# A six-phase encoder kernel: h kept in SBUF across three phases, first loads reordered, scores computed from parts

## The chip, the core and the metric

The kernel runs on one core of a Trainium2 chip. The metric is the device time of one execution in microseconds (us); the median of three runs is shown. All instruction times below come from one profiled execution of the kernel before.

## The reference, cut to what matters

```python
def trunk(x, mem, ...):
    h = rmsnorm(x, norm_g[l])
    proj = jnp.einsum('btd,de->bte', h, w_in[l])
    (g_q, g_k, g_v, g_lr, z_a, d_q, d_k, d_v, z_b, c_q, z_c, gate_in) = jnp.split(proj, offsets, axis=-1)
    o_a = gla_branch(g_q, g_k, g_v, g_lr, ...) * jax.nn.silu(z_a)
    o_b = diff_attention(d_q, d_k, d_v, ...) * jax.nn.silu(z_b)
    o_c = memory_cross_attention(c_q, mem, ...) * jax.nn.silu(z_c)
    branches = jnp.stack([o_a, o_b, o_c], axis=2)
    gates = jax.nn.sigmoid(gate_in.reshape(B, T, N_BRANCH, D))
    merged = jnp.sum(gates * jnp.einsum('btiw,iwd->btid', branches, w_branch[l]), axis=2)
    x = x + jnp.einsum('btd,de->bte', merged, w_out[l])
    return rmsnorm(x, final_norm_g)

def diff_attention(q, k, v, ...):           # 4 heads, two score maps of 64 channels each
    s = jnp.einsum('ibhqd,ibhkd->ibhqk', qblk, kh) + bias
    p = jax.nn.softmax(s, axis=-1)
    a = p[0] - lam * p[1]
    return jnp.einsum('bhqk,bhkv->bhqv', a, vh)
```

Two sequences of 512 and 2048 tokens (2560 in all) and 2 x 256 memory rows; D is 1024, all fp32, one layer. gla_branch is a gated linear attention that scans the tokens forward and backward.

## The kernel before

**Phases.** `build` runs six phases one after the other, with a barrier between them: `phase_project` (0 to 831 us), `phase_gla_forward` (835 to 1988), `phase_gla_backward` (1992 to 2312), `phase_diff` (2316 to 3151), `phase_cross` (3154 to 3276) and `phase_merge` (3279 to 3859). In a phase each engine runs a program written out by hand; semaphores tie them. SP issues nearly all loads and most stores in program order, each `dma_start` held back by the `wait_ge` ahead of it, so whatever stands behind a waiting load waits too. ACT issues the stores of the projection.

**Products.** Large products split each fp32 operand into a high and a low fp32r part and make three matmuls of 512 columns for one (`product3`, L114 to L116): high x high, low x high, high x low. The high part of a weight is a copy, the low one a subtraction on POOL.

**`phase_project`** goes through 5 chunks of 512 tokens. For each chunk ACT squares four x tiles (L243), DVE normalises them (L311), PE transposes them (L368), and ACT and DVE make h_hi (L252) and h_lo (L318). The units of a chunk are one "narrow" unit (the 32 gate-rank columns, in a 128-wide block), 8 "values" units whose weights stay resident, and 16 "stream" units, each with a 512 KB weight piece loaded by `load_piece` (L213) into one of two raw buffers (SLOTS = 2; the wait is on `lo_split`, two pieces back), split by DVE (L329) and POOL (L359). `load_x` (L208) of the next chunk's tiles stands between pieces on SP. A memory part of 8 units follows. hT_hi and hT_lo go to DRAM.

**`Dense`** computes the gate and z projections, 180 units of 24 products (L571), inside both GLA phases, interleaved with the scan. `load_h` loads a chunk of hT with 16 DMAs (L481, L482), `load_w` (L489) one weight block. Both phases take the chunks in order 0 to 4. `begin_transfers` issues the weight block 0, h chunk 0, weight blocks 1 to 3 and h chunk 1, after the phase's own loads.

**`phase_gla_forward`** has 20 tiles of 128 tokens; the o section of a tile (L766, L767) makes, for each of four heads in turn, att x v over 128 rows and Q x state over the head's 64 rows. PE waits for all constants (five loads, `consts_in`) and for DVE's copy of `sums` (L860) before its first matmul, the gate logits (L720).

**`phase_diff`** goes through groups of 4 turns, a turn being 128 queries of one head against T keys: 4 groups of the short sequence (T = 512), then 16 of the long one (T = 2048, 4 key chunks of 512 a turn). For a chunk PE computes the two score maps (L1360) as two fp32 matmuls of 64 rows each, which sit in the two row halves of the array; DVE adds the bias and takes the maximum (L1489), ACT takes the exponentials (L1436), POOL and DVE combine the two maps (L1319, L1323, L1519), PE transposes the result (L1374) and multiplies by v (L1385). The transposes are evacuated by ACT (L1430), every fourth by DVE (L1506). POOL scales q (`scale_q`). Whole heads of q and k are loaded at once; every engine first waits for all constants, `gain` (L1480) the last.

**`phase_cross`** and **`phase_merge`**: cross waits for all its constants before the first score (L1644). Merge adds 12 items (4 blocks of each branch, hi and lo, 24 loads of 256 KB a chunk, L1827 and L1828) weighted by gates; its first product waits for the first items.

## Time and profile before

| | |
|---|---|
| median of 3 runs | 3866.7 us (3863.07 to 3869.71) |
| the profiled execution: time, span | 3861.25 us, 3859.3 us |
| mean granted TensorE clock | 0.967 |
| busy: PE | 3568.4 us (92%), 17304 matmul records |
| busy: PE weight load | 2618.0 us (68%), overlaps PE |
| busy: DVE | 1881.8 us (49%) |
| busy: ACT | 1290.0 us (33%) |
| busy: POOL | 1246.5 us (32%) |
| moved by DMA | 542.81 MB, 141 GB/s |

The span runs from the first to the last instruction. PE busy includes stretches at the lower clock level, in which a matmul lasts about twice as long. An fp32 matmul shows as two records. In the rows, L12 is line 12 of the kernel before; PE is the matmul queue, SPq the issue of DMAs by SP, and the brackets give the idle time before an instruction and what ended it.

### The profile page before, as it was taken

How to read it: one execution, taken by the hardware profiler on the slowest of the kernel's cores; microseconds unless marked ns; L12 is line 12 of the kernel's file. 1: busy time of each engine (PE TensorE's matmuls, PEld its weight loads, DVE VectorE, ACT ScalarE, POOL GpSimd, SP SyncE). 2: the span in 40 equal slices, each digit the busy share in tenths (PEclk: the TensorE clock that was granted, in tenths of full speed). 3: DMA queues.
4: the chain of work that ended last, by engine and by line, in shares of the span. 5: the costliest groups of instructions: out<-in, count | busy, mean ns of one | idle time of the engine just before them, and what ended most of it. 6: DMA issues, size and time to landing. Idle time of an engine off the chain costs nothing. (4 is left out here: it accounts for less than half of the span.)

```text
span 3859.3 us, 46682 instructions
## 1 busy us (share of the span) xinstructions
PE 3568.4 (92%) x17304; PEld 2618.0 (68%) x17304; DVE 1881.8 (49%) x4161; ACT 1290.0 (33%) x2132; POOL 1246.5 (32%) x518
## 2 busy tenths in 40 slices
PE   6999999969999999999978986899999968899998
PEld 5778778758888888888866762344444435688887
DVE  4211211214333433433327786888888846555555
ACT  2111111113333333333322224455555535433332
POOL 2322321423332333233223324666666633200000
PEclk9999999989999999999989997999999989899999
DMA  5434434364343433433348873010110024866662
GB/s 178 147 140 148 153 142 145 136 215 146 124 161 113 161 124 119 150 127 115 110 151 279 284 214 132 28 39 28 39 36 17 17 96 164 309 205 216 214 206 98
DMA packets 304237, 542.81 MB, mean 141 GB/s; under 512 B 31595, under 2 KB 110571, under 8 KB 302604
## 3 DMA queue, kind: packets, MB, share of 16 engines
q1 hardware_dynamic: 258300, 469.29, 36.4%
q10 hardware_dynamic: 45712, 70.55, 5.1%
q8 instruction: 138, 2.26, 0.3%
q14 instruction: 87, 0.71, 0.1%
HBM read 380.07 MB, written 159.67 MB: 140 GB/s over the span
## 5 line engine op out<-in xcount | busy, mean ns | idle before, releaser
L555 POOL TENSOR_TENSOR glaf_w_lo<-glaf_raw,glaf_w_hi 128x1024 fp32r<-128x1024 f32 x140 | 351.8, 2513 | 807.1 <-ACT glaf_w_hi L525 807.1
L571 PE MATMUL glaf_dense_acc<-glaf_h_hi,glaf_w_hi 128*128 128x512 f32 x1120 | 451.8, 403 | 1.8 <-DMA glaf_h_lo<-scratch_hT_lo 1.8
L571 PE MATMUL glaf_dense_acc<-glaf_h_hi,glaf_w_lo 128*128 128x512 f32 x1120 | 439.8, 393 | 0.0
L571 PE MATMUL glaf_dense_acc<-glaf_h_lo,glaf_w_hi 128*128 128x512 f32 x1120 | 439.2, 392 | 0.0
L1489 DVE CUSTOM_DVE_ANT_0 diff_p<-diff_s_ps,diff_table 128x512 f32<-128x512 f32 x544 | 352.6, 687 | 108.2 <-PE diff_s_ps L1360 104.9
L359 POOL TENSOR_TENSOR proj_w_lo<-proj_raw,proj_w_hi 128x1024 fp32r<-128x1024 f32 x84 | 203.9, 2432 | 535.6 <-DVE proj_w_hi L329 535.6
L1360 PE MATMUL diff_s_ps<-diff_k,diff_q 64*128 64x512 f32 x1088 | 317.7, 664 | 32.6 <-DMA diff_gain<-in_diff_gain 23.0
L1319 POOL TENSOR_SCALAR diff_p<-diff_p,diff_ratio 128x1024 f32<-128x1024 f32 (+1 forms) x80 | 268.1, 3351 | 228.9 <-DVE diff_ratio L1516 228.8
L1385 PE MATMUL diff_oT_ps<-diff_aT,diff_v 128*128 128x512 f32 x544 | 290.3, 634 | 10.1 <-ACT diff_aT L1430 7.6
L114 PE MATMUL proj_acc<-proj_h_hi,proj_w_hi 128*128 128x512 f32 x672 | 269.0, 400 | 17.9 <-POOL proj_w_lo L359 17.9
L1436 ACT ACTIVATE diff_p<-diff_p,diff_neg_max 128x2048 f32<-128x2048 f32 (+1 forms) x160 | 278.4, 1741 | 15.0 <-DVE diff_neg_max L1499 14.9
L268 ACT ACTIVATE proj_out<-proj_acc 128x512 f32<-128x512 f32 x133 | 79.6, 598 | 601.0 <-PE proj_acc L116 601.0
L901 DVE COPY_PREDICATED glaf_att<-glaf_picked,glaf_att_ps 128x256 f32<-128x256 int32 x280 | 147.3, 526 | 270.2 <-PE glaf_att_ps L702 263.3
L1374 PEld LDWEIGHTS diff_t_ps<-diff_ident,diff_a 128*128 128x128 f32 x1088 | 131.6, 143 | 203.5 <-issue 147.0
L115 PE MATMUL proj_acc<-proj_h_lo,proj_w_hi 128*128 128x512 f32 x672 | 266.6, 397 | 0.0
L116 PE MATMUL proj_acc<-proj_h_hi,proj_w_lo 128*128 128x512 f32 x672 | 266.0, 396 | 0.0
L571 PEld LDWEIGHTS glaf_dense_acc<-glaf_h_hi,glaf_w_hi 128*128 128x128 f32 x1120 | 211.0, 188 | 45.9 <-issue 5.7
L571 PEld LDWEIGHTS glaf_dense_acc<-glaf_h_hi,glaf_w_lo 128*128 128x128 f32 x1120 | 210.8, 188 | 40.3
L571 PEld LDWEIGHTS glaf_dense_acc<-glaf_h_lo,glaf_w_hi 128*128 128x128 f32 x1120 | 211.2, 189 | 35.8
L868 DVE TENSOR_TENSOR glaf_K<-glaf_X,glaf_qk 128x1024 f32<-128x1024 f32 x80 | 118.1, 1477 | 219.1 <-ACT glaf_X L810 219.1
L1430 ACT ACTIVATE diff_aT<-diff_t_ps 128x512 f32<-128x512 f32 x208 | 122.8, 592 | 271.9 <-PE diff_t_ps L1374 271.1
L114 PE MATMUL merge_acc<-merge_br_hi,merge_w_hi 128*128 128x512 f32 x480 | 191.3, 398 | 22.6 <-DMA merge_br_lo<-scratch_item_lo 11.3
(199 smaller groups left out, 7055.2 us busy)
## 6 DMA issues: line engine op xcount, KB each, us to landing
glaf_raw<-in_w_zg SPq DMA_DIRECT2D x140, 512.0 KB, 3.6
proj_raw<-in_w_stream SPq DMA_DIRECT2D x80, 512.0 KB, 3.5
scratch_zg<-glaf_dense_out SPq DMA_DIRECT2D x140, 256.0 KB, 2.2
merge_raw<-in_w_br SPq DMA_DIRECT2D x120, 256.0 KB, 3.0
merge_gate<-scratch_zg SPq DMA_DIRECT2D x120, 256.0 KB, 3.6
scratch_featT<-proj_out ACTq DMA_DIRECT2D x80, 256.0 KB, 2.0
glab_raw<-in_w_zg SPq DMA_DIRECT2D x40, 512.0 KB, 4.9
merge_br_hi<-scratch_item_hi SPq DMA_DIRECT2D x60, 256.0 KB, 6.0
```

The costliest lines, as they stand in the source:

```text
L114: pe.matmul(out, a_hi, b_hi, start=first, stop=False)
L115: pe.matmul(out, a_hi, b_lo, start=False, stop=False)
L116: return pe.matmul(out, a_lo, b_hi, start=False, stop=last)
L359: pool.tensor_tensor(lo, raw[:, n % SLOTS], hi, ALU.subtract).then_inc(lo_split, 1)
L555: pool.tensor_tensor(self.w_lo[:, s], self.raw[:, u % self.RAW], self.w_hi[:, s], ALU.subtract).then_inc(self.lo_split, 1)
L571: done = pe.matmul(self.acc[:, u % self.BANKS], a, x, start=i == 0, stop=i == self.PER - 1)
L901: dve.copy_predicated(queries(att[:, :, :, :].rearrange("p z a t -> p (z a) t"), n, d), picked[:, d, n].rearrange("p (n m) -> p n m", m=ha ...
L1319: pool.tensor_scalar(p[:, o.slot, 1, half], p[:, o.slot, 1, half], ratio[:, o.slot:o.slot + 1], None, ALU.mult).then_inc(far_scaled, 1)
L1360: done = pe.matmul(s_ps[:, chunk % 2, i], q[r, n.head % 2, n.tile * P:(n.tile + 1) * P], k[r, n.head % 2, c * KC:(c + 1) * KC], start=True ...
L1385: pe.matmul(oT_ps[:, :], v[:, o.head % 2, kt], aT[:, unit % 2], start=kt == 0, stop=kt == o.nk - 1).then_inc(values_done, 1)
L1436: act.activation(p[:, o.slot, i, 0:o.T], p[:, o.slot, i, 0:o.T], ACT.Exp, bias=neg_max[:, o.slot, i:i + 1], scale=SLOPES[o.h], accum_out=s ...
L1489: dve.tensor_tensor_reduce(out=p[:, n.slot, i, c * KC:(c + 1) * KC], in0=s_ps[:, (n.c0 + c) % 2, i], in1=table[:, start:start + KC], scale ...
```

## The change

One diff touches all six phases.

- **h handed over.** `h` (hi and lo, two chunk buffers) is allocated once and passed to the projection and both GLA phases. `Dense` gets `held`, the number of chunks that it finds in place: forward takes the chunks as 4, 0, 1, 2, 3 and finds chunk 4 there; backward takes 3, 2, 4, 0, 1 and finds two. `load_w(0)` moves to the start of each pass. In forward, 20 products of the first unit are issued ahead of the wait for `sums`, and the waits for constants are split by constant.
- **Projection.** Resident weights come first and the narrow one last, in the order of pieces and of units; four raw buffers in place of two; ACT makes the high parts of the residents; in chunk 0 a values unit waits for its own x tile alone. The narrow unit becomes 16 matmuls (below), with `glr` stored as 64 rows and `w2` doubled to match. For the 8 blocks of d_q and d_k ACT writes the high part (q with its scale folded in), DVE a low part (`low_part`, 40 instructions of 128x512), and ACT stores that too (40 DMAs of 256 KB to `featT_lo`).
- **GLA forward.** The o section goes by pairs of heads: att, att, Q, Q. The gate logits contract 65 rows in place of 33.
- **Diff.** Scores from parts: two full-height fp32r matmuls and two half-height ones per chunk. q is loaded per group and k per chunk, 5 DMAs each (L1325 to L1346 of the changed kernel); `scale_q` goes; ACT does all transposes' evacuations; the bias table comes in three loads, with waits for each constant where it is used.
- **Cross and merge.** First q tile and memory first; merge's 24 first item loads are issued during cross (`Items`); merge starts with weights, gates and w_o.

```diff
 # phase_project
+            units += [("values", c, v, t) for v in range(2) for t in range(TT)]
             units += [("narrow", c, 0, 0)]
-            units += [("values", c, v, t) for v in range(2) for t in range(TT)]
...
-        STREAM, MEMC = N_FEAT, TOK // CH
+        STREAM, MEMC, RAW, NR = N_FEAT, TOK // CH, 4, 2 * RANK
...
             def load_piece(n):
-                if n >= SLOTS:
-                    sp.wait_ge(lo_split, n - SLOTS + 1)
-                sp.dma_start(raw[:, n % SLOTS], source(n)).then_inc(raw_in[n % SLOTS], 16)
+                if n >= RAW:
+                    sp.wait_ge(lo_split, n - RAW + 1)
+                sp.dma_start(raw_of(n), source(n)).then_inc(raw_in[n % RAW], 16)
...
+            def low_part(u):
+                i, n = units[u][2], part_units.index(u)
+                scale = HD ** -0.5 / SLOPES[i - DQ_BLOCK] if i < DK_BLOCK else 1.0
+                dve.wait_ge(evacuated, u + 1)
+                if n >= 2:
+                    dve.wait_ge(low_stored[n % 2], 16 * (n // 2))
+                dve.scalar_tensor_tensor(out_lo[:, n % 2], acc[:, u % BANKS], scale, out[:, u % OUTS], ALU.mult, ALU.subtract).then_inc(low_out, 1)
...
+                if kind == "narrow":
+                    both, high = acc[0:2 * NR, u % BANKS], acc[0:NR, u % BANKS]
+                    pe.matmul(both, wn[:, 0], h_hi[:, b, 0], start=True, stop=False)
+                    pe.matmul(high, wn[:, 0, 0:NR], h_lo[:, b, 0], start=False, stop=False)
+                    for k in range(1, KT):
+                        pe.matmul(high, wn[:, k, 0:NR], h_lo[:, b, k], start=False, stop=False)
+                        done = pe.matmul(both, wn[:, k], h_hi[:, b, k], start=False, stop=k == KT - 1)
 # phase_gla_forward
-                for h in range(H):
-                    r = head_rows(h)
-                    cols = slice(h // 2 * GV, (h // 2 + 1) * GV)
-                    pe.matmul(o_ps[:, h % 2, cols], att[:, h % 2, h // 2], v[:, b, h], start=True, stop=False)
-                    done = pe.matmul(o_ps[:, h % 2, cols], Q[r, 0, h // 2, INTER - 1], state[r, h // 2], start=False, stop=True)
+                for a in range(PAIRS):
+                    cols = slice(a * GV, (a + 1) * GV)
+                    for h in (2 * a, 2 * a + 1):
+                        pe.matmul(o_ps[:, h % 2, cols], att[:, h % 2, a], v[:, b, h], start=True, stop=False)
+                    for h in (2 * a, 2 * a + 1):
+                        r = head_rows(h)
+                        done = pe.matmul(o_ps[:, h % 2, cols], Q[r, 0, a, INTER - 1], state[r, a], start=False, stop=True)
 # phase_diff, scores
+                for i in range(2):
+                    pe.matmul(s_ps[:, chunk % 2, i], q_both[:, b, i, cols], k_both[:, key % KS, i], start=True, stop=False)
                 for i in range(2):
                     r = slice(HD * i, HD * (i + 1))
-                    done = pe.matmul(s_ps[:, chunk % 2, i], q[r, n.head % 2, n.tile * P:(n.tile + 1) * P],
-                                     k[r, n.head % 2, c * KC:(c + 1) * KC], start=True, stop=True)
+                    done = pe.matmul(s_ps[:, chunk % 2, i], q_high[r, b, cols], k_low[r, key % KS], start=False, stop=True)
 # phase_diff, ACT
-                if ku > 2:
-                    evacuate(o, 2)
+                for c in range(2, ku):
+                    evacuate(o, c)
 # phase_cross, SP
+            load_z(1)
+            items.load(sp, 0, 2 * H)
...
+                if c == 2:
+                    sp.wait_ge(stored[0], 32 * H)
+                    items.load(sp, 2 * H, 3 * H)
```

How the order of instructions moves at three places follows. First, PE in `phase_diff`, in a turn of the long sequence. Before:

```order
L1374 MATMUL diff_t_ps<-diff_ident,diff_a 128x128 x4
L1360 MATMUL diff_s_ps<-diff_k,diff_q 128x512 x2
L1385 MATMUL diff_oT_ps<-diff_aT,diff_v 128x512 x2
L1374 MATMUL diff_t_ps<-diff_ident,diff_a 128x128 x4
L1360 MATMUL diff_s_ps<-diff_k,diff_q 128x512 x2
```

And now (`q_both` holds q's high and low part in the two row halves, `k_both` k's high part twice):

```order
L1464 MATMUL diff_t_ps<-all_ident,diff_a 128x128 x4
L1448 MATMUL diff_s_ps<-diff_k_both,diff_q_both 128x512 x2
L1451 MATMUL diff_s_ps<-diff_k_low,diff_q_high 128x512 x2
L1475 MATMUL diff_oT_ps<-diff_aT,diff_v 128x512 x2
L1464 MATMUL diff_t_ps<-all_ident,diff_a 128x128 x4
```

The transposes and the products with v stand where they stood; each chunk's two score instructions have become four.

Second, PE in `phase_gla_forward`, the o section of one tile. Before:

```order
L766 MATMUL glaf_otd_ps<-glaf_v,glaf_att 128x128
L767 MATMUL glaf_otd_ps<-glaf_state,glaf_Q 128x128
L766 MATMUL glaf_otd_ps<-glaf_v,glaf_att 128x128
L767 MATMUL glaf_otd_ps<-glaf_state,glaf_Q 128x128
L766 MATMUL glaf_otd_ps<-glaf_v,glaf_att 128x128
L767 MATMUL glaf_otd_ps<-glaf_state,glaf_Q 128x128
L766 MATMUL glaf_otd_ps<-glaf_v,glaf_att 128x128
L767 MATMUL glaf_otd_ps<-glaf_state,glaf_Q 128x128
```

And now:

```order
L838 MATMUL glaf_otd_ps<-glaf_v,glaf_att 128x128 x2
L841 MATMUL glaf_otd_ps<-glaf_state,glaf_Q 128x128 x2
L838 MATMUL glaf_otd_ps<-glaf_v,glaf_att 128x128 x2
L841 MATMUL glaf_otd_ps<-glaf_state,glaf_Q 128x128 x2
L845 MATMUL glaf_otd_ps<-glaf_v,glaf_k_tok 64x128 x4
```

The same eight instructions alternate between the two shapes four times in place of eight.

Third, SP at the start of `phase_gla_backward`. Before:

```order
L977 DMA glab_o<-scratch_gla_o 128x512
L489 DMA glab_raw<-in_w_zg 128x1024
L481 DMA glab_h_hi<-scratch_hT_hi 128x512
L482 DMA glab_h_lo<-scratch_hT_lo 128x512
L481 DMA glab_h_hi<-scratch_hT_hi 128x512
```

And now:

```order
L562 DMA glab_raw<-in_w_zg 128x1024
L1049 DMA glab_qb<-scratch_qb 128x256
L1050 DMA glab_kb<-scratch_kb 128x256
L1051 DMA glab_dec<-scratch_decb 128x2
L1052 DMA glab_v<-scratch_gla_v 128x512
L1053 DMA glab_o<-scratch_gla_o 128x512
L1069 DMA glab_gain<-in_gla_gain 128x128
```

The first weight block (L489, now L562) is SP's first load of the phase; the 32 loads of h chunks at its start are gone.

## Rows read from the trace of the kernel before

**Rows 1.** Windows: length, busy us (instructions) of PE, PEld, DVE, ACT, POOL, clock, DMA share, GB/s.
```profile
860.00:1990.00 1130.00, 1123.89 (x6828) 916.41 (x6826) 419.45 (x558) 377.59 (x654) 348.05 (x139) 1.00 0.40 130
...
3275.00:3300.00 25.00, 11.62 (x28) 6.79 (x29) 4.66 (x8) 4.95 (x7) 0.00 (x0) 0.64 0.93 337
```

**Rows 2.** Timeline, PE, start of projection: start us, length us, line, operation, count, [idle before].
```profile
16.58 1.94 PE L368 MATMUL proj_tp<-proj_ident,proj_xn 128*128 128x128 f32 x8 [16.58 <-DVE proj_xn L311]
...
42.04 0.77 PE L114 MATMUL proj_acc<-proj_h_hi,proj_wn_hi 128*128 128x512 f32 x1 [2.85 <-issue]
```

**Rows 3.** Timeline, SP, the x load of a chunk boundary in the projection.
```profile
109.06 11.21 SPq L213 DMA_DIRECT2D proj_raw<-in_w_stream  x3
120.31 0.43 SPq L208 DMA_DIRECT2D proj_x<-in_x_all  x1
```

**Rows 4.** Timeline, PE, the same boundary, between chunks 0 and 1.
```profile
129.60 1.09 PE L368 MATMUL proj_tp<-proj_ident,proj_xn 128*128 128x128 f32 x8 [2.08 <-DVE proj_xn L311]
133.10 0.77 PE L114 MATMUL proj_acc<-proj_h_hi,proj_w_hi 128*128 128x512 f32 x1 [2.41 <-POOL proj_w_lo L359]
```

**Rows 5.** Windows, the same boundary.
```profile
129.00:137.00 8.00, 4.99 (x17) 4.00 (x18) 3.04 (x5) 1.08 (x2) 5.05 (x2) 0.64 0.47 157
```

**Rows 6.** Groups of 50 to 830 us, one line: | busy us, mean ns | idle before.
```profile
L114 PE MATMUL proj_acc<-proj_h_hi,proj_w_hi 128*128 128x512 f32 x672 | 269.0, 400 | 17.9 <-POOL proj_w_lo L359 17.9
```

**Rows 7.** Timeline, PE, the o section of one tile in phase_gla_forward.
```profile
1528.79 0.39 PE L571 MATMUL glaf_dense_acc<-glaf_h_hi,glaf_w_lo 128*128 128x512 f32 x1
1529.02 0.38 PE L766 MATMUL glaf_otd_ps<-glaf_v,glaf_att 128*128 128x128 f32 x2
1529.33 0.49 PE L767 MATMUL glaf_otd_ps<-glaf_state,glaf_Q 64*128 64x128 f32 x2
...
1532.25 0.66 PE L771 MATMUL glaf_otd_ps<-glaf_v,glaf_k_tok 128*64 128x128 f32 x8
```

**Rows 8.** Timeline, PE, where each later stage starts, and one gap inside phase_gla_backward.
```profile
845.53 1.19 PE L720 MATMUL glaf_z_ps<-glaf_decay_w,glaf_glr 33*128 33x512 f32 x1 [14.49 <-DVE glaf_sums L860]
...
2014.42 0.76 PE L571 MATMUL glab_dense_acc<-glab_h_hi,glab_w_hi 128*128 128x512 f32 x1 [14.66 <-DMA glab_h_lo<-scratch_hT_lo]
...
2048.94 0.47 PE L571 MATMUL glab_dense_acc<-glab_h_hi,glab_w_hi 128*128 128x512 f32 x1 [2.51 <-DVE glab_dense_out L540]
...
2328.35 6.34 PE L1360 MATMUL diff_s_ps<-diff_k,diff_q 64*128 64x512 f32 x16 [22.99 <-DMA diff_gain<-in_diff_gain]
...
3165.85 1.62 PE L1644 MATMUL cross_s_ps<-cross_kT,cross_q 128*128 128x256 f32 x3 [18.97 <-DMA cross_q<-scratch_featT]
...
3284.19 0.76 PE L114 MATMUL merge_acc<-merge_br_hi,merge_w_hi 128*128 128x512 f32 x1 [11.31 <-DMA merge_br_lo<-scratch_item_lo]
```

**Rows 9.** Timeline, PE, part of a long-head turn in phase_diff.
```profile
2704.37 0.60 PE L1374 MATMUL diff_t_ps<-diff_ident,diff_a 128*128 128x128 f32 x4
2704.90 1.13 PE L1360 MATMUL diff_s_ps<-diff_k,diff_q 64*128 64x512 f32 x4
2705.96 0.66 PE L1374 MATMUL diff_t_ps<-diff_ident,diff_a 128*128 128x128 f32 x4
...
2707.61 1.13 PE L1385 MATMUL diff_oT_ps<-diff_aT,diff_v 128*128 128x512 f32 x2
2708.57 0.60 PE L1374 MATMUL diff_t_ps<-diff_ident,diff_a 128*128 128x128 f32 x4
```

**Rows 10.** Timeline, PE, the closing gaps of two successive groups in phase_diff.
```profile
2494.80 0.66 PE L1374 MATMUL diff_t_ps<-diff_ident,diff_a 128*128 128x128 f32 x4 [1.67 <-DVE diff_a L1519]
...
2539.08 0.66 PE L1374 MATMUL diff_t_ps<-diff_ident,diff_a 128*128 128x128 f32 x4 [1.67 <-DVE diff_a L1519]
```

**Rows 11.** Windows, long heads.
```profile
2500.00:2600.00 100.00, 96.66 (x387) 42.65 (x385) 83.64 (x242) 54.44 (x71) 60.57 (x23) 1.00 0.10 38
```

**Rows 12.** Costliest groups of one such group of turns: two lines of ACT.
```profile
L1436 ACT ACTIVATE diff_p<-diff_p,diff_neg_max 128x2048 f32<-128x2048 f32 x8 | 16.0, 1997 | 0.0
...
L1430 ACT ACTIVATE diff_aT<-diff_t_ps 128x512 f32<-128x512 f32 x12 | 7.1, 592 | 14.3 <-PE diff_t_ps L1374 14.3
```

More of the change, by code:

```diff
@@ L135, in phase_project @@
         first_unit = [min(u for u, x in enumerate(units) if x[1] == c) for c in range(NC + 1)] + [len(units)]
-        pieces = [("narrow", 0, 0, 0)] + [("values", 0, v, col) for v in range(2) for col in range(COLS)]
+        pieces = [("values", 0, v, col) for v in range(2) for col in range(COLS)] + [("narrow", 0, 0, 0)]
         RESIDENT = len(pieces)
@@ L181, in phase_project, with in_parts @@
         evacuated = m.sem("evacuated")
+        low_out = m.sem("low_out")
+        low_stored = m.sems("low_stored", 2)
         stored = m.sems("stored", OUTS)
         block = m.block()
+        def in_parts(u):
+            kind, c, i, _ = units[u]
+            return kind == "stream" and c < MEMC and DQ_BLOCK <= i < CQ_BLOCK
+        part_units = [u for u in range(len(units)) if in_parts(u)]
         def source(n):
@@ L201, in split_into, with raw_of @@
             return w_hi[:, s], w_lo[:, s]
+        def raw_of(n):
+            return raw[:, n % RAW, :, 0:NR] if pieces[n][0] == "narrow" else raw[:, n % RAW]
         @block.sync
@@ L277, in evacuate, with high_resident @@
                     dst = memkT[i] if c == MEMC else featT[i, :, cols]
-                act.dma_start(dst, out[:, u % OUTS]).then_inc(stored[u % OUTS], 16)
+                act.dma_start(dst, out[0:2 * NR if kind == "narrow" else P, u % OUTS]).then_inc(stored[u % OUTS], 16)
+            def high_resident(n):
+                act.wait_ge(raw_in[n % RAW], 16 * (n // RAW + 1))
+                act.activation(split_into(n)[0], raw_of(n), ACT.Copy).then_inc(hi_resident, 1)
             square(0)
+            high_resident(0)
+            high_resident(1)
             square(1)
-            for n in range(TT):
-                high(n)
-                if n + 2 < TT:
-                    square(n + 2)
+            high(0)
+            high_resident(2)
+            high_resident(3)
+            square(2)
+            high(1)
+            high_resident(4)
+            high_resident(5)
+            square(3)
             for u, (kind, c, i, t) in enumerate(units):
@@ L347, in _ @@
                     split(n)
+                if u and in_parts(u - 1):
+                    low_part(u - 1)
                 j, r = divmod(at, 6)
@@ L566, in products @@
                     pe.wait_ge(self.evacuated, u - self.BANKS + 1)
-                if u in self.first_of:
-                    pe.wait_ge(self.h_in[b], 32 * KT * (index // self.buffers + 1))
+                if u in self.first_of and index >= self.held:
+                    loads = sum(i % self.buffers == b for i in range(self.held, index + 1))
+                    pe.wait_ge(self.h_in[b], 32 * KT * loads)
             a = (self.w_hi, self.w_hi, self.w_lo)[part][:, s, k]
@@ L1210, in phase_diff @@
         NORM_STEPS = 2 + RSQRT_STEPS
-        by_dve = [c % 4 == 3 for n in units for _ in range(G) for c in range(n)]
-        dve_before = [sum(by_dve[:i]) for i in range(len(by_dve) + 1)]
-        def wait_aT(engine, unit):
-            if by_dve[unit]:
-                engine.wait_ge(aT_dve, dve_before[unit] + 1)
-            else:
-                engine.wait_ge(aT_act, unit - dve_before[unit] + 1)
         class Turn:
@@ L1557, in _, with phase_cross @@
                     maximum(n)
-                if late and not (n.live and n.units > 3):
-                    evacuate(o, 3)
                 if e:
                     combine(e)
-def phase_cross(nc, featT, kT_dram, v_dram, ident_dram, zg, item_hi, item_lo):
+def phase_cross(nc, ident, items, featT, kT_dram, v_dram, zg, item_hi, item_lo):
     with ExitStack() as ctx:
```

400 lines of the change are left out of this document (237 added, 163 removed).

## The prediction

> **What bounds the kernel now.** I first read the windows by stage, to see which engine is full and at which clock. In the forward GLA pass PE is busy 1123.89 of 1130 us at full clock [rows 1]; time can go there only if PE gets less to do. Around the first 25 us of merge it is busy 11.62 us at a mean clock of 0.64, with the DMA share at 0.93 [rows 1]: there loads decide. Then I read the timeline of PE at the start of each stage for the idle time and its releaser [rows 2, 8], and at a chunk boundary of the projection [rows 3 to 5]. Last come the long heads of diff, where PE is busy 96.66 of 100 us, DVE 83.64, POOL 60.57 and ACT 54.44 [rows 11]: PE bounds, and DVE is second with little room. So the kernel is PE-bound with a dozen stalls between, and PE pays for a stall twice, since it also comes back at half clock: after the stall at 133.10 the pitch of products is 0.57 and then 0.43 us, and the window shows 0.64 [rows 4, 5].
>
> **The sum, by places.** All against the span of 3859.3 us.
>
> *Start of the projection.* The first transposes start at 16.58 and the first product at 42.04, after all four x tiles [rows 2]. Now the first values unit needs one tile and four weight pieces. Transposes 1.94 us plus the two h parts put the tile at about 21; the high parts of the weights move to ACT and no longer queue behind DVE's normalising. I take 23, so -19. The ends are -21 (nothing but the tile) and -8 (POOL's low parts come at today's rhythm).
>
> *Chunk boundaries.* SP's load of the next x tile is issued only at 120.31, after 11.21 us of waiting for a raw buffer [rows 3]; PE then lacks 2.08 and 2.41 us [rows 4], and of 8 us a share of 0.36 goes to the clock, 2.9 us [rows 5]. With four buffers SP is two units further ahead, more than the stall. Five boundaries x 7.4 = -37. DVE's new low parts fall in stream units and have room: POOL and DVE wait there. The wait new on PE (a bank whose low part must be taken) is three units old by then: nothing.
>
> *Memory part.* Of the idle time ahead of these products, 17.9 us [rows 6], five boundaries explain 12; the rest, 5.9, is weight pieces late in the memory part: -6 with deeper buffers.
>
> *Narrow unit.* Eight matmuls fewer in each of five chunks, at a pitch of 0.23 from 1528.79 to 1529.02 [rows 7], is -9. But they now alternate between 64 and 32 columns, 15 changes a unit. The nearest row with changes of shape is the o section, where a pair of records takes 0.40 ((1532.25 - 1529.02) / 8) against 0.21 for two records of 0.107, which is the pitch of transposes (0.43 for four [rows 9], with the change 0.53): 0.1 to 0.2 a change, of which I take the o section's 0.2. 75 x 0.2 = +15, so +6 in sum; it is the same kind of change though not the same shapes. Ends -9 and +6.
>
> The Trainium skill, "TensorEngine Tiling (Array Packing)", Key Properties, says that a change of tiling mode (not of tile) drains TensorE; by that rule the narrow unit and the split scores each pay, and the o section gains. It speaks against two parts of this change; the sum by it is the sum here, as the rows already carry the price of 0.2. No row before shows a change of columns alone.
>
> *Projection to forward GLA.* PE is idle 14.49 us to 845.53, released by DVE's copy of `sums`, which waited for the last constant [rows 8]. The logits need only `decay_w` and the gates now, and 20 products follow at once; their weights come fourth in SP's queue. How early the weights arrive is not shown; I take two thirds of the idle time: -10. Ends -3 and -15.
>
> *o section, 20 tiles.* Eight pairs of 0.40 = 3.2 us [rows 7]. Now four changes x 0.2, four att products x 0.21, and the Q products, two row halves at once, 2 x 0.21: 2.1. PE is full here, so 20 x 1.1 = -22 (ends -16, if the two halves don't run at once, and -24). The logits' 65 rows no longer run beside their neighbours: 20 x 0.1 = +2.
>
> *Start of backward GLA.* The idle 14.66 us ended by h_lo [rows 8] go: both h chunks are there, and the weights are first in the queue: -14. Inside the phase about half of the eight gaps (2 to 4 us each, as the one at 2048.94) follow the first two h loads, gone: -8.
>
> *Diff, start.* 22.99 us, released by `gain`, the last of the constants [rows 8]. q, k and the near part of the table are still loaded, now as 10 DMAs for one turn in place of whole heads: -5, and -2 in the short heads.
>
> *Diff, long heads.* From 2704.37 four transposes take 0.53 with the change to row halves, of which 0.43 are theirs; the scores take 1.06 to 2705.96; the next transposes have 0.06 of exposed weight load either way: 1.16 a chunk. A change to a full-height matmul costs no drain (0.96 for two fp32 matmuls of 512 columns, 2707.61 to 2708.57) [rows 9]. Now: two full matmuls x 0.23, change 0.2, one pair at 0.23, change back 0.1: 0.99. Saved 0.17 x 256 chunks = -44. Groups repeat every 44.28 us, with a closing gap of 1.67, fourteen times [rows 10]; the period should fall to 41.5. Ends: the pair one after the other, +0.23 a chunk, in all +14; and no load exposed, -60. DVE at 37.0 of 44.28 us loses four copies and stays near 83% of the shorter period. ACT takes those over: 16.0 us of exponentials and 16 x 0.59 of copies [rows 12], 26.5 of 41.5 in all. POOL loses `scale_q`, which was off the path.
>
> *Cross and merge.* Cross waits 18.97 us for its q [rows 8], issued fifth; now it is first: -5 (the barrier and the transfer stay). Merge waits 11.31 us for item low parts [rows 8] and then runs at 0.64 [rows 1]. 24 loads are now done during cross; what remains is the first weights: -17, ends -8 and -22. The new wait in cross (`stored[0]`, then four items) is on SP, with the z load and stores behind it, and they have a whole chunk's time.
>
> Sum: -19 - 37 - 6 + 6 - 10 - 22 + 2 - 14 - 8 - 7 - 44 - 5 - 17 = **-181**. Span 3678, time 3680 (the profiled execution took 1.95 more than its span, 3861.25). The median of the runs is 5.4 above the profiled execution, so I forecast **3685 us**.
>
> **Rivals.**
> 1. *The long heads give nothing.* Either the fp32r row halves run one after the other, or DVE's bias chain takes over as the bound when PE gets faster. For: DVE is at 84%, and no row shows fp32r in row halves. Against: fp32 halves run at once (four records in 0.96). Time 3685 + 44 = 3729, up to 3743. Chance 0.15.
> 2. *The boundary stalls stay.* Something besides x is late (DVE's `norm` behind more `low_part`), so the 37 us stay: 3722. Against: the window shows DVE idle over half of the time there. Chance 0.08.
> 3. *First loads only swap places.* At each of the five stage starts the barrier and one DMA chain remain, and half of the 51 us stays: 3711. Chance 0.12.
> 4. *Narrow changes are free*: 3670. Chance 0.08.
> 5. *Slower: ACT holds up diff.* The fourth transposes' copy now stands behind both exponentials (2.0 us each [rows 12]) in ACT's queue; PE's product with v waits for it, and PE's own queue with the next scores behind that. If one exponential comes in the way in each of 64 turns, 128 us are lost: 3813, still faster. From 2.9 us a turn the change is slower, and with both, 4.0 x 64 = 256, it is 3941. For: ACT's third copy today already stands there, and PE's waits on copies are short. ACT has 35% room in the mean, so I give it 0.03.
> 6. *The hold of h or items is not effective* (the loads wait on the same semaphore as before, or the buffers cost a wait elsewhere): 3720, chance 0.02.
>
> **The numbers.** The forecast has 0.52. Its own range, from the ends of the terms, is 3655 to 3710. To leave out no more than 2 in 10 I take 3645 to 3735, which holds rivals 1 to 4 with nearly all of their chance. A measurement of this kernel tells 0.2%, some 8 us, from no change; only rival 5 comes near or above it. Faster by over 0.2%: 0.96; within 0.2%: 0.015; slower: 0.025.
>
> **What would show it.** In the profile after: a first product near 23 us; no gap over 1 us at the four inner chunk boundaries and clock 1.00 in them; the narrow unit at about 6.7 us or 3.7 (rival 4); the o section at 2.1 us; backward GLA's first dense product right after its first deltas; groups of long turns every 41.5 us (44.3 is rival 1), with PE busy still above 95%; merge's first product some 5 us after cross. A wait of PE's products with v on ACT's copy, over 1 us a turn, would be rival 5. The forecast is wrong if the span is over 3730, or if it is right in sum with two of these places wrong.

## The result and the profile after

The changed kernel takes **3696.06 us** (median of 4 runs, 3694.17 to 3701.03) against 3865.26 us before: a ratio of 0.9563, 95% interval 0.9546 to 0.9579. I had forecast 3685 us with a range of 3645 to 3735. The profiled execution has a span of 3695.6 us, 163.7 less than before, where the sum had said 181. One execution of the changed kernel in run 9 took 5738.88 us at a mean granted clock of 0.556, and every comparison leaves it out. Measured between PE's first and last instructions of each stage (the last row goes on to the end of the span), the time went here:

| stretch of PE's timeline | before, us | after, us | change | forecast |
|---|---|---|---|---|
| start to the first product | 42.0 | 23.1 | -19.0 | -19 |
| projection, first to last product | 789.0 | 743.7 | -45.3 | -37 |
| on to the first dense product of forward GLA | 25.3 | 14.5 | -10.8 | -10 |
| forward GLA from there | 1131.5 | 1120.0 | -11.5 | -20 |
| on to PE's last instruction of backward GLA | 317.5 | 292.2 | -25.4 | -22 |
| wait ahead of diff | 23.0 | 20.0 | -3.0 | -5 |
| diff | 818.5 | 789.6 | -28.9 | -46 |
| wait ahead of cross | 19.0 | 12.3 | -6.7 | -5 |
| cross and merge | 693.5 | 680.2 | -13.3 | -17 |

The page of the changed kernel, busy time by engine: PE's share rises, but its busy time falls by only 83 us of the 164; the rest was idle time.

```profile
PE 3485.7 (94%) x17264; PEld 2628.7 (71%) x17264; DVE 1858.3 (50%) x4128; ACT 1332.0 (36%) x2205; POOL 1221.9 (33%) x510
```

PE's timeline at the starts of the stages, after (to be held against [rows 2, 8]):

```profile
23.09 0.78 PE L118 MATMUL proj_acc<-proj_wv_hi,h_hi 128*128 128x512 f32 x1
...
48.52 1.97 PE L428 MATMUL proj_tp<-all_ident,proj_xn 128*128 128x128 f32 x8 [6.49 <-DVE proj_xn L365]
...
773.84 2.04 PE L789 MATMUL glaf_z_ps<-glaf_decay_w,glaf_glr 65*128 65x512 f32 x2 [7.07 <-DMA glaf_decay_w<-in_w]
781.26 0.79 PE L643 MATMUL glaf_dense_acc<-h_hi,glaf_w_hi 128*128 128x512 f32 x1 [5.37 <-POOL glaf_w_lo L626]
798.36 0.69 PE L807 MATMUL glaf_z_ps<-glaf_sums,glaf_L_hi 128*128 128x384 f32 x1 [9.65 <-ACT glaf_X L884]
...
1912.70 1.22 PE L1112 MATMUL glab_o_ps<-glab_state,glab_qb 64*128 64x128 f32 x8 [11.46 <-DVE glab_state L1149]
...
1914.91 0.80 PE L643 MATMUL glab_dense_acc<-h_hi,glab_w_hi 128*128 128x512 f32 x1
...
2213.40 1.19 PE L1448 MATMUL diff_s_ps<-diff_k_both,diff_q_both 128*128 128x512 f32 x2 [19.98 <-DMA diff_k_low<-scratch_featT_lo]
...
3015.37 2.90 PE L1747 MATMUL cross_s_ps<-cross_kT,cross_q 128*128 128x256 f32 x6 [12.32 <-DMA cross_kT<-scratch_memkT]
...
3135.98 0.79 PE L118 MATMUL merge_acc<-items_br_hi,merge_w_hi 128*128 128x512 f32 x1 [10.47 <-DVE merge_w_lo L2120]
```

The 14.66 us ahead of the first dense product of backward GLA are gone: it follows the phase's first scan matmuls with no idle time. The wait ahead of those scan matmuls stays, 11.46 us at 1912.70 (9.67 before), and the forecast had no term for it. At the other starts a wait remains, with another releaser: merge no longer waits for items but 10.47 us for the split of its first weights. Two rows are new stalls: 6.49 us at 48.52, where the first x tile of chunk 1 is late, and 9.65 us at 798.36. SP issues the load of that x tile at 31.14, behind a weight piece, and ACT can square the tile only from 38.60.

The windows of the changed kernel for the whole steady projection, and for four successive groups of the long heads and a later one (length, busy us with instruction counts of PE, PEld, DVE, ACT, POOL, then clock, DMA share, GB/s):

```profile
60.00:760.00 700.00, 700.00 (x3164) 575.55 (x3163) 171.93 (x413) 118.59 (x203) 213.96 (x88) 1.00 0.48 169
```

```profile
2452.54:2494.15 41.61, 39.94 (x171) 21.26 (x171) 34.19 (x99) 26.28 (x35) 27.52 (x11) 1.00 0.12 35
2494.15:2540.38 46.23, 44.56 (x171) 23.97 (x171) 33.55 (x99) 26.39 (x35) 27.54 (x11) 0.89 0.20 58
2540.38:2581.96 41.58, 39.91 (x171) 21.26 (x171) 34.21 (x99) 26.28 (x35) 27.54 (x11) 1.00 0.13 40
2581.96:2625.82 43.86, 40.48 (x170) 21.30 (x171) 34.18 (x99) 26.29 (x35) 27.49 (x11) 1.00 0.36 110
...
2708.95:2755.23 46.28, 44.62 (x171) 23.93 (x171) 33.55 (x99) 26.39 (x35) 27.51 (x11) 0.89 0.11 34
```

In the projection PE is busy 700 of 700 us at full clock: every boundary stall is gone [rows 4, 5]. In diff a plain group takes 41.58 us, as forecast (41.5). But three of this profile take 46.2 at a clock of 0.89, and the one in which the head changes takes 43.9. These are what the forecast of diff lacked. A closer look at the group that begins at 2494, in 2 us windows:

```profile
2492.00:2494.00 2.00, 0.48 (x2) 0.00 (x0) 1.87 (x5) 1.23 (x2) 1.13 (x1) 1.00 1.01 288
2494.00:2496.00 2.00, 1.85 (x10) 1.17 (x11) 0.13 (x2) 1.16 (x2) 2.00 (x1) 0.87 1.00 308
2496.00:2498.00 2.00, 2.00 (x8) 1.24 (x6) 1.27 (x4) 2.00 (x4) 1.85 (x2) 0.50 0.99 288
```

The idle time of 1.67 us ahead of the group's first transposes is the one of [rows 10]; before the change the full clock held across it 14 times. Now the clock falls to 1.2 GHz after 4 of the 14: three times for about 10 us, which costs 4.6, and once, at 2927, for about 7, which costs 3.3.

How the scores now lie in a turn of the long heads (PE's timeline, to be held against [rows 9]), the o section (against [rows 7]) and a part of the narrow unit:

```profile
2703.88 0.60 PE L1464 MATMUL diff_t_ps<-all_ident,diff_a 128*128 128x128 f32 x4
2704.24 0.70 PE L1448 MATMUL diff_s_ps<-diff_k_both,diff_q_both 128*128 128x512 f32 x2
2704.87 0.50 PE L1451 MATMUL diff_s_ps<-diff_k_low,diff_q_high 64*128 64x512 f32 x2
2705.30 1.98 PE L1475 MATMUL diff_oT_ps<-diff_aT,diff_v 128*128 128x512 f32 x4
```

```profile
1288.03 0.60 PE L838 MATMUL glaf_otd_ps<-glaf_v,glaf_att 128*128 128x128 f32 x4
1288.57 0.49 PE L841 MATMUL glaf_otd_ps<-glaf_state,glaf_Q 64*128 64x128 f32 x4
1288.99 0.71 PE L838 MATMUL glaf_otd_ps<-glaf_v,glaf_att 128*128 128x128 f32 x4
1289.63 0.49 PE L841 MATMUL glaf_otd_ps<-glaf_state,glaf_Q 64*128 64x128 f32 x4
1290.05 0.66 PE L845 MATMUL glaf_otd_ps<-glaf_v,glaf_k_tok 128*64 128x128 f32 x8
```

```profile
78.12 0.39 PE L450 MATMUL proj_acc<-h_hi,proj_wn 128*64 128x512 f32 x1
78.35 0.40 PE L451 MATMUL proj_acc<-h_lo,proj_wn 128*32 128x512 f32 x1
...
81.58 0.39 PE L454 MATMUL proj_acc<-h_hi,proj_wn 128*64 128x512 f32 x1
81.81 0.38 PE L428 MATMUL proj_tp<-all_ident,proj_xn 128*128 128x128 f32 x2
```

From the start of the transposes to the end of the scores a chunk takes 0.36 + 1.06 us where it took 0.53 + 1.06: the saving of 0.17 stands between the transposes and the scores. Within the 1.06 the two full-height matmuls take 0.63 and the pair in the row halves 0.43. The trace puts the two starts of the pair 0.004 us apart (2704.870 and 2704.874), so the halves run at once; how the 0.43 divides into a change of shape and the products no run shows. The o section takes 2.02 us in place of 3.23, and 20 of them give -24. The narrow unit takes 3.69 us, 16 times 0.23: its 15 changes of width cost nothing.

### The profile page after: what moved, and what is told of

The parts are those of the page before. It is cut to its first block and busy times, and to the rows that moved or that the text cites. A ratio compares the mean times of both kernels' runs of the same rounds, so it can differ in the third digit from the quotient of the medians.

```text
span 3695.6 us, 46898 instructions
## 1 busy us (share of the span) xinstructions
PE 3485.7 (94%) x17264; PEld 2628.7 (71%) x17264; DVE 1858.3 (50%) x4128; ACT 1332.0 (36%) x2205; POOL 1221.9 (33%) x510
## 5 line engine op out<-in xcount | busy, mean ns | idle before, releaser
L643 PE MATMUL glaf_dense_acc<-h_hi,glaf_w_hi 128*128 128x512 f32 x1120 | 452.7, 404 | 5.4 <-POOL glaf_w_lo L626 5.4
L643 PE MATMUL glaf_dense_acc<-h_hi,glaf_w_lo 128*128 128x512 f32 x1120 | 440.2, 393 | 0.0
L643 PE MATMUL glaf_dense_acc<-h_lo,glaf_w_hi 128*128 128x512 f32 x1120 | 439.7, 393 | 0.0
L118 PE MATMUL proj_acc<-h_hi,proj_w_hi 128*128 128x512 f32 x672 | 262.8, 391 | 0.0
L120 PE MATMUL proj_acc<-h_hi,proj_w_lo 128*128 128x512 f32 x672 | 261.6, 389 | 0.0
L119 PE MATMUL proj_acc<-h_lo,proj_w_hi 128*128 128x512 f32 x672 | 261.5, 389 | 0.0
L643 PEld LDWEIGHTS glaf_dense_acc<-h_hi,glaf_w_hi 128*128 128x128 f32 x1120 | 211.4, 189 | 51.2 <-POOL glaf_w_lo L626 6.9
L643 PEld LDWEIGHTS glaf_dense_acc<-h_hi,glaf_w_lo 128*128 128x128 f32 x1120 | 211.4, 189 | 41.2
L643 PEld LDWEIGHTS glaf_dense_acc<-h_lo,glaf_w_hi 128*128 128x128 f32 x1120 | 211.7, 189 | 36.0
L1448 PE MATMUL diff_s_ps<-diff_k_both,diff_q_both 128*128 128x512 f32 x544 | 204.9, 459 | 31.0 <-DMA diff_k_low<-scratch_featT_lo 24.0
```

Of the source, the lines that this page charges most:

```text
L118: pe.matmul(out, a_hi, b_hi, start=first, stop=False)
L119: pe.matmul(out, a_hi, b_lo, start=False, stop=False)
L120: return pe.matmul(out, a_lo, b_hi, start=False, stop=last)
L643: done = pe.matmul(self.acc[:, u % self.BANKS], a, x, start=i == 0, stop=i == self.PER - 1)
L1448: pe.matmul(s_ps[:, chunk % 2, i], q_both[:, b, i, cols], k_both[:, key % KS, i], start=True, stop=False)
```

## The experiments

The ratio of each run is taken to the kernel before on the same chip. "Span" is that of the profiled execution, the changed kernel's is 3695.6, and where nothing else is said a difference in span is against that one profile. Diff alone, with the changed kernel's scores and waits, takes 778.2 to 791.1 us in nine profiles, so I also give the stage that an edit touches.

**1. The projection's raw buffers alone, in the kernel before** (RAW is 4).

```diff
-                if n >= SLOTS:
-                    sp.wait_ge(lo_split, n - SLOTS + 1)
-                sp.dma_start(raw[:, n % SLOTS], source(n)).then_inc(raw_in[n % SLOTS], 16)
+                if n >= RAW:
+                    sp.wait_ge(lo_split, n - RAW + 1)
+                sp.dma_start(raw[:, n % RAW], source(n)).then_inc(raw_in[n % RAW], 16)
```

> The kernel before, with four raw buffers for weight pieces in the projection in place of two, nothing else. Theory (the x loads were late because SP stood in a wait for a raw buffer): the idle times of 2.1 and 2.4 us and the half-clock stretch at the five chunk boundaries go, and the stalls of the memory part too; first to last product of the projection falls from 789 us to about 746, the span from 3859 to 3816. Rival (what was late was DVE or POOL work of the boundary, or the gain came from the other edits of the projection): the gaps stay, span 3859 within 4 us.

Measured: 3810.42 us, ratio 0.9864 (0.9849 to 0.9878), span 3815.7; first to last product 744.1 us. SP's timeline and the window of the first boundary in this kernel:

```profile
109.12 0.43 SPq L208 DMA_DIRECT2D proj_x<-in_x_all  x1
```

```profile
124.00:140.00 16.00, 16.00 (x77) 13.32 (x76) 3.37 (x5) 2.89 (x5) 6.50 (x4) 1.00 0.37 131
```

The x load is issued at 109.12 where it was at 120.31 [rows 3], and the boundary has no idle time. The theory stands: from first to last product the deeper buffering takes off 44.9 us (the span 43.6), 27% of the whole. By the medians, 3810.42 against 3864.53, it is 54 us; the profiled execution was the slowest of the four of this kernel (the other three took 3810), and where the other 10 us lie is not shown. The run also says that the rest of the projection's edits give nothing net between first and last product (744.1 against 743.7): the narrow unit's -9 is used up by the stall of 6.49 at 48.5, the lower clock behind it, and the transposes of two x tiles, which now fall behind the first product.

**2. The o section in its old order**, in the changed kernel (the loop of the kernel before put back, as in the diff of the change).

> The changed kernel with the o section of the forward GLA pass in its old order (att, Q for one head after the other). Theory (a change between full height and row halves costs 0.2 us, and two Q products in different halves run at once): the section goes back from 2.02 to 3.23 us, 20 times, +24 us in a phase in which PE is full: 3720. Rival (PE waits for the scan there, so the time saved became idle time elsewhere): under +8 us, 3696 to 3703.

Measured: 3721.77 us, ratio 0.9631 (0.9615 to 0.9647), span 3721.1: +25.5 (+25.7 by the medians), of which 22 lie in forward GLA. The theory stands.

**3. h not held.**

```diff
-        self.held = held
+        self.held = 0
```

> The changed kernel, in which both GLA passes load all their h chunks again, into the same two buffers and in the changed order of chunks. Theory (holding h is worth the start of the backward pass and part of its inner gaps): forward start +5 (16 more transfers ahead of the rest), backward start +10 to +14, inner gaps +5: 3716 to 3728. Rival (the early first weight block was what mattered, h is loaded in the same time): under +8, up to 3703.

Measured: 3727.42 us, ratio 0.9644 (0.9629 to 0.9658), span 3727.1: +31.5. PE's timeline of this kernel at both starts:

```profile
794.76 0.77 PE L643 MATMUL glaf_dense_acc<-h_hi,glaf_w_hi 128*128 128x512 f32 x1 [18.72 <-DMA h_lo<-scratch_hT_lo]
...
1941.76 0.76 PE L643 MATMUL glab_dense_acc<-h_hi,glab_w_hi 128*128 128x512 f32 x1 [12.39 <-DMA h_lo<-scratch_hT_lo]
```

Forward now waits 18.72 us for h_lo (its first dense product stands 13.5 us later than at 781.26), and the stall at 798 shrinks to 7.5. Backward gets back the 12.39 us ahead of its first product and its last product comes 20 us later after forward's last one than in the changed kernel. The theory stands, at its upper end, with most of the 31 in backward; the forward start cost more than it said, 13.5 us in place of 5.

**4. Merge's first items loaded by merge.** The two `items.load` of cross are left out, and merge issues the 24 loads between its first weights and gates, as the kernel before did.

> The changed kernel with merge's first 24 item loads at the start of merge, in the order that the kernel before had, and none during cross. Theory (the early items are worth merge's first stalls): cross runs 3 us faster (107 in place of 110), merge's first product waits on items again and its later stalls and half-clock stretches come back, from first product to end 575 in place of 560: +12 net, 3708. Rival (the load of the first weights bounds merge's start either way): within 4 us of 3696.

Measured: 3713.73 us, ratio 0.9609 (0.9591 to 0.9626), which is +18 by the medians. The four executions lie in two pairs, 3706.71 and 3708.5, 3718.95 and 3719.81, and the profiled one is the slowest: span 3717.7, +22, of which 20 lie in cross and merge together. PE's timeline after its first product:

```profile
3149.80 0.47 PE L118 MATMUL merge_acc<-items_br_hi,merge_w_hi 128*128 128x512 f32 x1 [2.41 <-DVE merge_w_lo L2123]
...
3171.71 0.79 PE L118 MATMUL merge_acc<-items_br_hi,merge_w_hi 128*128 128x512 f32 x1 [7.48 <-DVE merge_w_lo L2123]
```

The windows of merge's first 50 us, with early items and in this run:

```profile
3135.98:3185.98 50.00, 48.47 (x201) 39.05 (x202) 43.22 (x44) 29.13 (x47) 20.27 (x8) 0.95 0.85 292
```

```profile
3142.08:3192.08 50.00, 38.28 (x126) 27.40 (x127) 22.84 (x29) 20.44 (x33) 12.30 (x5) 0.78 0.93 336
```

Right in direction, somewhat small in size (+12 expected), and right on merge itself: 565.8 us from first to last product, 549.7 with early items, 565.2 in the kernel before. It was wrong on cross, which took 113 us against 110. The first wait hardly differs (11.19 us here, 10.47 with early items, 11.31 in [rows 8]). The gain of the early items lies behind it, where PE now waits 2.41 and 7.48 us for the split of later weights and the clock is 0.78 in place of 0.95. I read from this that the early items free DMA time for those weights.

Cross is no measure of the item loads: in the profiles of all kernels it takes 106.9 to 107.3 us where the clock is at the lower level for some 7 us of it, 109.5 to 111.0 at 10 to 14 us, and 113.1 at 20. The code of the kernel before gives both 107.0 (its own profile) and 110.2 (run 1).

**5. Weight blocks ahead of the h chunk in forward GLA.**

```diff
         self.load_w(sp, 1)
-        for index in range(self.held, self.buffers):
-            self.load_h(sp, index)
         self.load_w(sp, 2)
         self.load_w(sp, 3)
+        for index in range(self.held, self.buffers):
+            self.load_h(sp, index)
```

> The changed kernel with SP issuing weight blocks 2 and 3 of the forward GLA pass ahead of the 16 loads of the h chunk that is needed much later. Theory (ACT stands in its queue in the wait for weight block 2, issued at 786.5 behind those loads and landed at 796.9, with the scan's work behind it, and PE waits for that): the new gap of 9.7 us at 798 goes with its half-clock stretch of some 2 us: span -10 to -12, about 3685. Rival (the DMA engines are full there, share 0.94, and other loads are late in its place): under 4 us, above 3691.

Measured: 3685.61 us, ratio 0.9533 (0.9515 to 0.9551), span 3684.4: -11.2. Forward GLA from its first dense product takes 1110.4 us in place of 1120.0. The rows that had led to the theory, SP's and ACT's timelines of the changed kernel, and then the window of the stall in this run:

```profile
786.50 2.15 SPq L562 DMA_DIRECT2D glaf_raw<-in_w_zg  x2
```

```profile
796.88 1.06 ACT L596 ACTIVATE glaf_w_hi<-glaf_raw 128x1024 fp32r<-128x1024 f32 x1 [11.06 <-DMA glaf_raw<-in_w_zg]
797.84 0.85 ACT L884 ACTIVATE glaf_X<-glaf_z_ps 128x384 f32<-128x384 f32 x2
```

```profile
781.00:799.00 18.00, 17.57 (x73) 14.25 (x73) 9.88 (x11) 8.14 (x14) 7.89 (x3) 0.90 0.73 258
```

PE is busy 17.57 of these 18 us; in the changed kernel it was 8.09. A smaller wait of 2.37 us, for DVE, appears at 816. So the stall was an in-order queue at work twice: the weight load stood behind 16 loads on SP, and the scan's exponentials stood behind the wait for that weight on ACT.

**6. Scores ahead of the transposes where a group opens.**

```diff
+                ahead = bool(o) and o.quarter == 0 and nu > 0
+                if ahead:
+                    scores(n, 0)
                 for c in range(2):
                     if c < ku:
                         transposes(o, c)
-                    if c < nu:
+                    if c < nu and not (ahead and c == 0):
                         scores(n, c)
```

> The changed kernel, in which PE in the turn that opens a group's transposes issues the next turn's first score chunk (1.05 us) ahead of them. Theory (the 1.67 us of idle time at each closing are a wait for DVE's last combination, and the half-clock stretches of 4.6 us after some of them follow from the idle time): the gap falls to about 0.6, 16 times, -17, and the three to five half-clock stretches go, -14 to -23: 3660 to 3668. Rival 1 (DVE, 83% busy, is the chain that sets the group's period): the gap reappears elsewhere, period 41.6, 3696. Rival 2 (the half-clock stretches have nothing to do with this gap): 3679 or so, with the stretches still there.

Measured: 3666.18 us, ratio 0.9478 (0.9457 to 0.95), span 3663.5: -32. PE's timeline at a closing, and the window of all long heads:

```profile
2491.11 1.09 PE L1464 MATMUL diff_t_ps<-all_ident,diff_a 128*128 128x128 f32 x8 [0.77 <-DVE diff_a L1608]
```

```profile
2325.00:2946.00 621.00, 603.28 (x2560) 323.72 (x2559) 525.09 (x1471) 400.63 (x529) 415.74 (x152) 1.00 0.19 57
```

The idle time falls to 0.77, the group from 41.58 to 40.58 us, which is 16 us in all, and the clock is 1.00 over 621 us, where the changed kernel shows 0.97 (559 us, its long heads). The theory stands and both rivals fall: the gap was part of the period, and the half-clock stretches went with it. That this is no chance of one profile is seen over all of them. In nine profiles with the gap of 1.67 us the clock fell after 21 of 126 closings. In the two with 0.77 (this run and run 12) it fell after none of 27. Diff takes 754.6 us here, and 761.7 in run 12.

**7. Without the pair of row halves.** The products of q's high with k's low part are left out, and the full-height matmuls close the accumulation.

> The changed kernel without the two half-height score matmuls of each chunk: the product of q's high part with k's low part is left out of the scores. Theory (PE bounds the long heads, with DVE close behind): the pair costs 0.42 us, so PE would have 41.6 - 16 x 0.42 = 34.9 us of work a group, less than DVE's 34.2 with its waits; the period becomes 36 to 37, -75 us in all, 3620, and DVE's busy share goes to over 0.92. Rival (DVE or ACT already set the period): it stays at 41 or so.

Measured: 3633.57 us in one run, span 3631.5: -64. A plain group takes 38.2 to 39.2 us. The window of 100 us of long heads:

```profile
2500.00:2600.00 100.00, 82.86 (x357) 50.01 (x356) 89.16 (x254) 68.37 (x92) 73.70 (x27) 1.00 0.26 79
```

Of the 6.7 us a group taken off PE about 3 came back as time: neither 36.5, as the theory put it, nor 41. (The theory also called PE's 34.9 us of work less than DVE's 34.2; they are nearly equal.) PE is now idle 17%; in this window it waits 7.9 us for DVE's bias step and 5.9 for DVE's last combination, and DVE is busy 0.89. I read from this that DVE's chain is a bound about 3 us below the present 41.6, without a run of its own to show it. Rival 1 of the prediction had a real wall in it, only further off.

**8. The narrow unit grouped by width** (7 matmuls of 64 columns, 8 of 32, 1 of 64).

> The changed kernel, whose narrow unit issues the 64-column matmuls together and the 32-column ones together (2 changes of width in place of 15). If a change of width cost something beyond what the records show, the unit would fall below its 3.70 us (16 x 0.23); if, as its length suggests, it is free, 3.70 stays.

Measured: 3688.8 us in one run, span 3686.9; first to last product of the projection 744.5 us, against 743.7. The unit is not shorter, 3.70 us: changes of width are free in this kernel. The 8.7 us less in the span come from diff (778.8 us, 10.8 less), where one half-clock stretch follows a closing in place of four.

**9. The changed kernel once more**, as the reference of the next three.

> The changed kernel as it is, on the same chip as the three below, as their reference: 3695 within 6 us. If the half-clock stretches of the long heads are chance events, their places differ from the first profile; if they come with the program, they stand in the same groups.

Measured: 3696.17 us (median of three), ratio 0.9553 (0.9537 to 0.9569), span of the profiled execution 3685.2, with diff at 778.7 us. One long group takes 46.2 us, at another place than those of the first profile, and the plain ones take 41.6 again:

```profile
2664.80:2711.00 46.20, 44.57 (x170) 23.93 (x170) 33.53 (x99) 26.38 (x35) 27.42 (x11) 0.89 0.20 58
```

So the stretches come by chance and not at fixed places: the nine profiles with this gap have one to four each, at changing groups. It is not chance alone, since the two profiles with the old scores (the kernel before and run 1) have none after 28 closings with the same 1.67 us; why they have none is not shown. One profile alone can put diff some 11 us too high or too low.

**10. h chunks handed out in portions.** After each dense unit SP issues 4 of a chunk's 16 loads, and forward starts with weight blocks 1 to 3, as in run 5.

```diff
         self.load_w(sp, 1)
-        for index in range(self.held, self.buffers):
-            self.load_h(sp, index)
         self.load_w(sp, 2)
         self.load_w(sp, 3)
+        self.pending += [(index, k) for index in range(self.held, self.buffers) for k in range(0, KT, 2)]
...
                 if index < len(self.chunks):
-                    self.load_h(sp, index)
+                    self.pending += [(index, k) for k in range(0, KT, 2)]
+            if self.pending:
+                index, k = self.pending.pop(0)
+                self.load_h(sp, index, (k, k + 1))
```

> The changed kernel with each h chunk's 16 loads handed out 4 at a time, one portion after each dense unit, instead of in one run, and weight blocks 2 and 3 first at the start of forward. Theory (a run of 16 loads holds SP and the DMA engines, and weight blocks and tiles behind it come late): the forward gap of 9.7 goes as in the run with weights first (-11), and most of the 13 us of gaps inside the backward pass go too: 3672 to 3678. Rival (backward is full of transfers whatever their order, DMA share 0.8): only the forward part, about 3684.

Measured: 3660.47 us, ratio 0.9467 (0.9451 to 0.9483), span 3659.1: -36 against run 9 by the medians. Forward takes 1112.1 us in place of 1127.4 (first to last matmul) and backward 266.5 in place of 280.7, 30 us together; backward's gaps over 1 us fall from 13.4 us in five to 3.8 in two. The other 6 us are less than diff varies by from profile to profile. Run 5's order alone left forward at 1117.8 and backward at 283.9, so that 23 of the 30 us belong to the portions. The theory stands and gave somewhat too little: every run of 16 loads had cost something, not only the first.

**11. Three loads a piece in diff in place of five.**

```diff
-                for i in range(2):
-                    for half in range(2):
-                        sp.dma_start(k_both[HD * half:HD * (half + 1), s, i].bitcast(FP32), featT[DK_BLOCK + h, HD * i:HD * (i + 1), cols]).then_inc(k_in[s], 16)
+                for half in range(2):
+                    sp.dma_start(k_both[HD * half:HD * (half + 1), s].bitcast(FP32), featT[DK_BLOCK + h, :, cols].rearrange("(i p) t -> p i t", i=2)).then_inc(k_in[s], 16)
...
```

> The changed kernel with q's and k's parts in diff loaded by 3 DMAs a piece in place of 5. Theory (at the three changes of long heads PE waits for k because SP needs 3 us for the five issues of a chunk, more than PE's 2.4 us): the groups at a change of head fall from about 43.5 to 42 us or less, -4 to -6 in all, and the first score of diff comes 2 us earlier: 3688. Rival (the transfers, not their issue, are late): within 2 us of no change.

Measured: 3697.54 us, ratio 0.956 (0.9545 to 0.9576): no difference from run 9. The groups at a change of head take 42.7, 44.1 (48.7 with a half-clock stretch in it) and 42.2 us, where run 9 has 43.1, 43.7 and 42.8, and diff's first score comes after 19.8 us of waiting, not 18. A miss, and the rival stands: the transfers are late, not their issue. At the second change of head SP needs 1.9 us for a chunk in place of 3.0, but the last k load, issued at 2614.60, lands only at 2624.01, 9.4 us later, while PE waits for it. In the first profile of the changed kernel the waited-for loads took 4.2 and 4.5 us to land. The DMA share in 2615 to 2625 is over 1.0 here and 0.85 there. Whether more than the single turn of notice would help was not tried.

**12. Runs 6, 10 and 11 together.**

> Scores ahead of the transposes at a group's opening, h loads spread and weights first, and 3 loads a piece, together. If the gains add up (-32, -20, -7): 3637, and PE over 96% busy. If one of them had only moved a wait that another one meets again: 3645 to 3655.

Measured: **3636.82 us** (3635.49 to 3641.47), ratio 0.9408 (0.9394 to 0.9422). PE is busy 3463.6 of 3635.9 us, 95% and not the 96% expected. The gains nearly add up: -30 (run 6) and -36 (run 10) against -59, by medians. This version beats both kernels.

## Why the forecast was right, and which steps were off

The time, 11 us above the forecast, lies in the range, and the likeliest case was the right one. That the sum came within 17 us of the span is partly luck: the projection gave 8 us more than the sum said, where the narrow unit had been put 15 us too dear, and this hides part of the 8 and 17 us that forward GLA and diff did not give. Of the places named as signs of being wrong, one did not come about: merge's first product stands 10.5 us after cross and not 5. Step by step:

- **Start of the projection (-19):** right; the first product stands at 23.09. Not foreseen was the next wait, 6.49 us at 48.5, for a tile whose load still stands behind a weight piece on SP.
- **Boundaries and memory part (-43):** right in mechanism and size, 44.9 by the stage in run 1.
- **Narrow unit (+6):** wrong. The step that failed is taking the o section's 0.2 us a change for changes of column width. The unit takes 3.69 us: -9, as rival 4 had it. Here the rule of the Trainium skill ("TensorEngine Tiling (Array Packing)", Key Properties) that a change of tiling mode drains TensorE and the trace part: between 64 and 32 columns at full height nothing shows, between full height and row halves it is 0.1 to 0.2 us.
- **Forward GLA (-22 +2):** wrong in size, -11.5 for -20. The o section itself measured -24, and run 2 gives it back. The sum missed a stall of 9.65 us that the change itself makes. I had counted what the early weight block brings and not which later weight block the h loads now push back, and who waits behind it on ACT.
- **Start and inside of backward GLA (-22):** right, -25.4; run 3 gives 20 of it to holding h. The sum left out the 10 us of waiting ahead of the phase's scan, which stayed (9.67 before, 11.46 after).
- **Diff, the scores (-44):** right in its sum, 0.17 us a chunk and 41.58 us a group against a forecast of 41.5, but not in all its parts. The two full-height matmuls take 0.63 us and not 0.46, the transposes ahead of them 0.36 and not 0.43, and no change back shows; the differences cancel, which is luck. The halves run at once, so rival 1 did not come about, and PE's waits on ACT's copies total 4.6 us on the page, so rival 5 did not either. What failed is what I took as fixed: that the closing gap costs 1.67 us and nothing else. Diff gave 28.9 us for 46. Four half-clock stretches took back 17 us in the first profile and groups in which loads come late about 6 (1.1 to 2.3 us each), while the short heads gave some 5 more than forecast. In run 9, with one such stretch, diff gives 39.8. One reading was off as well: the 0.96 us of [rows 9] are one fp32 matmul in two records, not two matmuls. No term changes by it.
- **Cross and merge (-22 with the wait ahead of cross):** -19.9 in sum, and not where I put it. The 11 us of waiting ahead of merge's first product stayed, with the weights' split as releaser; the gain is in the stalls and the clock behind it, 15.5 us within merge (run 4). Cross itself took 3 us more in this profile. Run 4 shows that this is the clock, 12.6 us at the lower level in place of 6.7, and not the item loads.

## What to carry to other kernels

When a load is moved forward in a queue, list what is behind it now and which engine stands in an in-order wait for each of those; the stall of 9.65 us was of this kind by run 5, and handing out such loads in portions took 30 us off the two GLA phases in run 10. A short idle time that repeats is worth filling even where it looks cheap, since the clock may fall after it. And buffers that let the loading queue run further ahead of a wait can be worth more than all the arithmetic saved: two more raw buffers gave 45 of 164 us.

## What the runs showed of the hardware that I had not expected

- fp32r matmuls of 64 rows in the two row halves run at once: the two of a pair start 0.004 us apart, and from a pair of 512 columns to the next instruction it is 0.43 us.
- A change between 64 and 32 columns costs nothing between matmuls of 512 columns (0.23 us each, 16 in 3.69 with 15 changes, 3.70 with 2).
- After the same idle time of 1.67 us the clock fell to 1.2 GHz for 7 to 10 us after 21 of 126 closings of the changed scores, at changing places, and after none of 28 in the two profiles of the old ones; with 0.77 us of idle time it held after all of 27.
- Splitting a chunk's 16 loads of 256 KB into portions gave 23 us in the two GLA phases (run 10 against run 5), 6 of them in a forward phase whose DMA share is only 0.40 [rows 1], without moving a byte less.
- Fewer and larger loads were no faster: with 3 in place of 5 a piece, issue took 1.9 us in place of 3.0, and the last k load of a chunk took 9.4 us to land in place of 4.5.
